# Expert gate and up products with the weight tiles held stationary and the tokens moving

## What is computed

```python
def expert_block(args):
    xb, e = args
    return (jax.nn.silu(xb @ w_gate[e]) * (xb @ w_up[e])) @ w_down[e]
```

## Time and profile before

| | |
|---|---|
| median of 3 runs | 1424.87 us |
| the profiled execution | 1424.23 us |
| its span, first to last instruction | 1422.5 us |
| PE busy | 1219.2 us, 86% of the span |
| weight loads busy | 919.9 us, 65% |
| DVE busy | 875.8 us, 62% |
| ACT busy | 739.7 us, 52% |
| mean granted TensorE clock | 0.949 |
| bytes moved | 285.04 MB |

### The profile page before, as it was taken

The page is one execution under the profiler, slowest core; times in us unless marked ns, Lnnn a source line. Parts: engine busy times, 40 slices in busy tenths (PEclk is TensorE's granted clock), DMA queues, the critical chain, the costliest instruction groups (busy, mean ns, idle before and its releaser), DMA issues. The chain is left out here.

```text
span 1422.5 us, 18503 instructions
## 1 busy us (share of the span) xinstructions
PE 1219.2 (86%) x6174; PEld 919.9 (65%) x6174; DVE 875.8 (62%) x951; ACT 739.7 (52%) x850; POOL 149.2 (10%) x140
## 2 busy tenths in 40 slices
PE   3799999999999999699824999999999999999700
PEld 2597678768767876488723666666666666666500
DVE  4334534453455345533375888888888888888525
ACT  5234344344334344522205777777777777777422
POOL 0000000000000000010002111111111111111043
PEclk9999999999999999899956999999999999999855
DMA  4121010111011110454345999999999999999256
GB/s 135 32 75 45 17 44 15 44 31 43 12 35 43 29 44 0 167 182 143 111 192 203 362 398 390 397 392 396 396 388 393 397 396 393 390 399 393 109 161 220
DMA packets 80460, 285.04 MB, mean 200 GB/s; under 512 B 12280, under 2 KB 38904, under 8 KB 55856
## 3 DMA queue, kind: packets, MB, share of 16 engines
q1 hardware_dynamic: 68384, 242.09, 45.0%
q0 software_dynamic: 8464, 30.02, 6.9%
q10 hardware_dynamic: 3584, 12.58, 2.2%
HBM read 255.01 MB, written 29.66 MB: 200 GB/s over the span
## 5 line engine op out<-in xcount | busy, mean ns | idle before, releaser
L1428 DVE TENSOR_TENSOR m_wl<-raw,m_wh 128x2048 fp32r<-128x2048 f32 x192 | 437.3, 2289 | 88.5 <-ACT m_wh L1372 86.2
L1372 ACT ACTIVATE m_wh<-raw 128x2048 fp32r<-128x2048 f32 x192 | 367.7, 1918 | 150.5 <-PE m_py L277 50.7
L289 PE MATMUL a_pj<-zh,a_wh 128*128 128x348 f32 (+1 forms) x432 | 112.0, 358 | 0.0
L289 PE MATMUL a_pj<-zl,a_wh 128*128 128x348 f32 (+1 forms) x432 | 111.8, 358 | 0.0
L289 PE MATMUL a_pj<-zh,a_wl 128*128 128x348 f32 (+1 forms) x432 | 110.7, 355 | 0.0
L275 PE MATMUL m_py<-m_wh,m_hh 128*96 128x512 f32 x256 | 103.6, 405 | 8.2 <-DVE m_hl L1457 8.2
L275 PE MATMUL m_pg<-m_wh,m_xh 128*96 128x512 f32 x256 | 104.6, 409 | 5.8 <-DVE m_xl L1432 4.4
L275 PE MATMUL m_pu<-m_wh,m_xh 128*96 128x512 f32 x256 | 102.6, 401 | 0.0
L277 PE MATMUL m_pg<-m_wh,m_xl 128*96 128x512 f32 x256 | 102.1, 399 | 0.0
L276 PE MATMUL m_py<-m_wl,m_hh 128*96 128x512 f32 x256 | 101.9, 398 | 0.0
L276 PE MATMUL m_pg<-m_wl,m_xh 128*96 128x512 f32 x256 | 101.8, 398 | 0.0
(11 more groups left out here) (259 smaller groups left out, 2139.1 us busy)
## 6 DMA issues: line engine op xcount, KB each, us to landing
raw<-in_w_gate_dram SPq DMA_DIRECT2D x64, 1024.0 KB, 8.1
raw<-in_w_up_dram SPq DMA_DIRECT2D x64, 1024.0 KB, 8.7
raw<-in_w_down_dram SPq DMA_DIRECT2D x64, 1024.0 KB, 7.7
a_raw<-in_w_in_dram SPq DMA_DIRECT2D x26, 512.0 KB, 3.8
yrows<-m_ys ACTq DMA_DIRECT2D x32, 384.0 KB, 7.7
yrows<-o_blank POOLq DMA_DIRECT2D x22, 384.0 KB, 4.5
a_cb<-negcum SPq DMA_DIRECT2D x8, 520.0 KB, 3.8
n_x<-in_x_dram SPq DMA_DIRECT2D x8, 512.0 KB, 3.2
```

Of the source, the lines that this page charges most:

```text
L289: mm = nc.tensor.matmul(out, w[:, k, 0:m], z[:, k, at:at + n], start=n_pass == 0, stop=n_pass == PASSES - 1)
L1372: nc.scalar.activation(wh[s][:], raw[j][:], ACT.Copy).then_inc(S["w_hi"], 1)
L1428: nc.vector.tensor_tensor(wl[s][:], raw[j][:], wh[s][:].bitcast(F32), ALU.subtract).then_inc(S["w_lo"], 1)
```

## The change

In gate and up the operands swap sides. The weights become stationary: of the 512 columns of a slice, tile m takes the columns m, m+4, m+8, ... (128 of them, every fourth), so that output partition p holds hidden column 4p+m, as `w_down` lies. The tokens move. Their high and low parts lie side by side in one buffer `xs`, and one matmul of `wh` against both gives 192 columns (96 for the high tokens, 96 for the low ones). A second matmul, of `wl` against the high part alone, adds its 96 columns to the first half. Per slice and for each of the four tiles m that is a pair of matmuls with two weight loads; before it was three matmuls with three weight loads for the whole slice.

The result has hidden columns on partitions already, so the four transposes to `phid` go. The two halves of each sum have to be added: ACT copies the second half out of PSUM (`low_g`, `low_u`), DVE adds the first half to it. Silu then works on the sum in SBUF. All these operations have 128 partitions and 384 elements.

```diff
-                            mm = three_passes(nc, out[:], xh[u][:, k * BLK:(k + 1) * BLK], xl[u][:, k * BLK:(k + 1) * BLK],
-                                              wh[s][:, n], wl[s][:, n], k == 0, k == KD - 1)
+                            for m in range(MT):
+                                n = slice(b * DE + m, (b + 1) * DE, MT)
+                                nc.tensor.matmul(out[:, spot(m):spot(m) + 2 * BLK], wh[s][:, n],
+                                                 xs[u][:, k, :, :].rearrange("p c n -> p (c n)"), start=k == 0 and m % 2 == 0, stop=False,
+                                                 skip_group_check=True)
+                                mm = nc.tensor.matmul(out[:, spot(m):spot(m) + BLK], wl[s][:, n], xs[u][:, k, 0, :],
+                                                      start=False, stop=k == KD - 1, skip_group_check=True)
...
-                        pe.wait_ge(S["silu_done"], N + 1)
+                        pe.wait_ge(S["g_summed"], N + 1)
                         into_hidden(N, u, pg, GATE, shift)
-                    if shift != FIRST:
                         pe.wait_ge(S["h_done"], N + 1)
-                        pe.wait_ge(S["h_lo"], N)
-                        for t in range(DE // P):
-                            mm = nc.tensor.transpose(phid[:, t * BLK:(t + 1) * BLK], hid[:, t * P:(t + 1) * P],
-                                                     c.ident[0:BLK, 0:BLK])
-                        mm.then_inc(S["h_turned"], 1)
-                    if shift != CLOSING:
                         into_hidden(N, u, pu, UP, shift)
```

On ACT (step N; `high` is the copy of one unit's high part):

```diff
                     if shift != CLOSING:
-                        for kind in GATE:
-                            high(N, u, kind + shift)
+                        high(N, u, GATE[0] + shift)
+                    if shift != FIRST:
+                        act.wait_ge(S["unit_used"], used(N - 1, UP[1], shift_of(N - 1) if isinstance(N, int) else INNER))
+                        act.wait_ge(S["h_done"], N)
+                        nc.scalar.activation(by_spot(low_u), sides(pu[:])[1], ACT.Copy).then_inc(S["u_copied"], 1)
+                        act.wait_ge(S["g_summed"], N + 1)
+                        nc.scalar.activation(act_g[:], act_g[:], ACT.Silu).then_inc(S["silu_done"], 1)
+                    if shift != CLOSING:
+                        high(N, u, GATE[1] + shift)
                         x_high(N, u)
...
                     if shift != FIRST:
+                        act.wait_ge(S["h_done"], N + 1)
...
+                        nc.scalar.activation(hh[:], hid[:], ACT.Copy).then_inc(S["h_hi"], 1)
                         for kind in DOWN:
                             high(N, u, kind + shift)
                     if shift != CLOSING:
                         act.wait_ge(S["unit_used"], used(N, GATE[1], shift))
-                        act.wait_ge(S["h_done"], N + 1)
-                        nc.scalar.activation(act_g[:], pg[:], ACT.Silu).then_inc(S["silu_done"], 1)
...
+                        act.wait_ge(S["g_summed"], N + 1)
+                        nc.scalar.activation(by_spot(low_g), sides(pg[:])[1], ACT.Copy).then_inc(S["g_copied"], 1)
```

More of the change, by code:

```diff
@@ L1249, in experts @@
         xg = [c.sb(ctx, f"{tag}_xg{s}", [BLK, D], F32) for s in range(2)]
-        xh = [c.sb(ctx, f"{tag}_xh{s}", [P, KD * BLK], F32R) for s in range(2)]
-        xl = [c.sb(ctx, f"{tag}_xl{s}", [P, KD * BLK], F32R) for s in range(2)]
+        xs = [c.sb(ctx, f"{tag}_xs{s}", [P, KD, 2, BLK], F32R) for s in range(2)]
         ids = [c.sb(ctx, f"{tag}_ids{s}", [BLK, 1], I32) for s in range(2)]
-        act_g = c.sb(ctx, tag + "_act_g", [BLK, DE], F32)
-        hid = c.sb(ctx, tag + "_hid", [BLK, DE], F32)
+        act_g = c.sb(ctx, tag + "_act_g", [P, DE // P * BLK], F32)
+        hid = c.sb(ctx, tag + "_hid", [P, DE // P * BLK], F32)
+        low_g = c.sb(ctx, tag + "_low_g", [P, DE // P * BLK], F32)
+        low_u = c.sb(ctx, tag + "_low_u", [P, DE // P * BLK], F32)
         hh = c.sb(ctx, tag + "_hh", [P, DE // P * BLK], F32R)
@@ L1375, in x_high @@
                     act.wait_ge(S["x_turned"], N + 2)
-                    nc.scalar.activation(tiles4(xh[u][:]), banks4(px[:]), ACT.Copy).then_inc(S["x_hi"], 1)
+                    nc.scalar.activation(part(u, 0), banks4(px[:]), ACT.Copy).then_inc(S["x_hi"], 1)
                 def y_out(i, u, k, down):
@@ L1395, in step @@
                     if shift != FIRST:
+                        act.wait_ge(S["h_done"], N + 1)
+                        if not (isinstance(N, int) and N == 1):
+                            act.wait_ge(S["unit_used"], used(N - 1, DOWN[1]))
+                        nc.scalar.activation(hh[:], hid[:], ACT.Copy).then_inc(S["h_hi"], 1)
                         for kind in DOWN:
@@ L1418, in _ @@
                 dve.sem_inc(S["x_lo"], 1)
+                dve.sem_inc(S["g_summed"], 1)
+                dve.sem_inc(S["u_summed"], 1)
                 dve.sem_inc(S["h_done"], 1)
@@ L1431, in x_low @@
                     dve.wait_ge(S["x_hi"], N + 1)
-                    nc.vector.tensor_tensor(tiles4(xl[u][:]), banks4(px[:]), tiles4(xh[u][:]).bitcast(F32),
-                                            ALU.subtract).then_inc(S["x_lo"], 1)
+                    nc.vector.tensor_tensor(part(u, 1), banks4(px[:]), part(u, 0).bitcast(F32), ALU.subtract).then_inc(S["x_lo"], 1)
                 def hidden(k):
[L1436 to L1441, removed]
+                    dve.wait_ge(S["u_copied"], k + 1)
+                    dve.wait_ge(S["h_lo"], k + 1)
+                    nc.vector.tensor_tensor(by_spot(hid), sides(pu[:])[0], by_spot(low_u), ALU.add).then_inc(S["u_summed"], 1)
+                    dve.wait_ge(S["u_summed"], k + 2)
+                    dve.wait_ge(S["silu_done"], k + 1)
+                    nc.vector.tensor_tensor(hid[:], hid[:], act_g[:], ALU.mult).then_inc(S["h_done"], 1)
                 def step(i, u, N, shift):
                     if shift != CLOSING:
-                        for kind in GATE:
-                            low(N, u, kind + shift)
+                        low(N, u, GATE[0] + shift)
                     if shift != FIRST:
@@ L1449, in step @@
                     if shift != CLOSING:
+                        low(N, u, GATE[1] + shift)
                         x_low(N, u)
```

36 lines of the change are left out of this document (19 added, 17 removed).

## The result

The changed kernel takes 2052.37 us (median of 4 runs, 2049.10 to 2053.20) against 1424.80 for the kernel before (now the median of 4 runs): ratio 1.4395, 95% interval 1.437 to 1.442. It is slower, as forecast. But the forecast was 1508 with a range up to 1970, so the size was missed by far.

What follows compares the result with a forecast made beforehand. PE was taken to bound the experts stage, with loads replacing columns as its pace: 1424.2 + 92.2 for gate and up - 8.6 for transposes = 1507.8, so 1508 us; own range 1495 to 1530, all cases 1494 to 1970.

Steps and rivals of the forecast that it cites:

- Rival C: Chain through ACT and DVE to xl becomes later than PE by 0.5 us a step: 16 us, 1524 us; chance 0.08.
- PE's former share: Sign in the profile after: the busy share of gate and up weight loads rises above 70%.
- the price of a load of 128 neighbouring columns: On PE in gate and up, 0.110 us a load sets the pace: +92.2 us over 64 products.
- Rival B: Gate and up loads hide and columns decide; the gain ends at the DMA engines: 1419 us; chance 0.06.
- I take no cost: Gate and up loads reading every fourth column, 16 bytes apart, stay at 0.110 us each, with nothing added for the stride.
- the upper bound: The stride at most doubles a gate or up load to 0.220 us: up to +451 us over 4096 loads.
- Rival A: The stride doubles gate and up loads to 0.220 us: 1959 us, step 34.6 us; chance 0.34 including values between.
- the clock: Granted clock in the experts stage: the forecast is wrong if it falls below 1.00; no time was assigned to it.
- the DMA engines as the next limit: If loads hide, DMA at share 1.01 limits the gain to at most 1% of the 573 us of 32 steps.

Runs made afterwards that it cites:

- block_columns: The changed kernel with each weight tile made of 128 neighbouring columns and w_down's rows fetched to match, so no load has a stride: 1537.92 us, ratio 1.0799.
- xl_first: The kernel before, without the swap, with DVE making the tokens' low part xl ahead of the hidden product: 1415.62 us, ratio 0.9942.
- moving_stride2: The kernel before, with the 512 moving weight columns of a gate or up matmul taken as every second one of two slices: 1761.43 us.
- wide_moving: The changed kernel, stride-four loads kept, with each gate and up matmul moving 512 token columns in place of 192 or 96: 2026.3 us.
- hid_in_a_row: The kernel before, without the swap, with the hidden product written without a stride and w_down's rows fetched to match: 1416.76 us, ratio 0.9952.

## Why the prediction was wrong

**Right: what bounds the kernel and which way it goes.** PE sets the pace in both kernels, the loads take over from the columns, and slower was forecast at 0.94. ACT and DVE stayed hidden, in block_columns too, whose step is close to the one forecast. Rival C is out by that run. (The 70% that the forecast calls PE's former share is that of the weight loads in the earlier trace rows; it is 95% after.)

**Right: the price of a load of 128 neighbouring columns.** 0.110 from three places of the trace; 0.1115 in block_columns, whose step of 20.61 us stands against the 20.5 of the forecast. The forecast of 1508 was in effect one for that kernel (1537.92), and even there 1530, the top of its own range, was passed, because of the clock in the first two steps. Rival B (loads that hide) is out by the same run.

**Wrong: "I take no cost" for the stride.** This is the step that failed. The argument was that a load already takes 0.86 ns per column and that a reader at half its full rate would keep up. It counted rates by columns. What is paid is 16-byte lines, at 1.82 ns each: 128 neighbouring columns have 32 lines (58 ns by that price, below the load's own 111), and every fourth column has 128 (233 ns). 4096 loads at +0.12 us is some 500 us.

**Wrong: the upper bound.** Rival A doubled the load, 0.220, to 1959 us. The mechanism and the place were right, its chance of 0.34 too low, and its size short: 0.2334 instead of 0.220 is 55 us, and the clock came on top. Its bound was a factor taken from DVE's writes. A bound was in reach from PE's own rows: 512 neighbouring float32 columns are 128 lines and take 0.231 us, and if lines were what is paid there, a load with 128 lines would cost about the same.

**Wrong: the clock was left out of the sum.** I named it only as something that would break the forecast. It cost 45 to 50 us in the token transposes and the down products. The loads of the changed kernel lost nothing to it, since their lines cost the same at either clock; those of block_columns lost 26 us in its first two steps. With slow loads and narrow moving operands this belonged beside rival A.

**Partly right: the DMA engines as the next limit.** They move the same bytes. That they would have come next in rival B is argued and not shown. At a share of 1.01 there was room for a step at least 1.3% shorter (17.91 to 17.67 us in xl_first), where I allowed 1%; where they do stop isn't known. The share is a poor measure of what is left: block_columns had 345 GB/s, as forecast (341), but at a share of 0.97 and not the 0.88 that the forecast scaled from the rate.

**Not settled.** Why a line costs 1.82 ns in a load and 1.77 in a moving operand, and why stride eight costs 0.006 us more than stride four. On the moving side only strides of one and two were run. The runs with strides of two, three and eight, moving_stride2 and wide_moving were run once each; what is read from them are spacings that repeat hundreds of times in a trace, but for the 17 at half clock in moving_stride2.

## What to carry to other kernels

Before operands are swapped, count three things for each side: moving columns, weight loads, and the 16-byte lines that each access touches. In this kernel's float32r products, the time from one matmul to the next was close to the largest of their prices. A stride of two in a stationary tile was nearly free, and a stride of four doubled the cost of a load; on the moving side a stride of two already doubled the cost of a matmul. If the layout asks for every fourth column, permute the rows of the next weight matrix in its fetch instead: that took 514 us off, and the other fetch cost nothing that could be measured (hid_in_a_row has it and is as fast as xl_first). The swap did not pay even so: block_columns is 8% slower than the kernel before.

An engine that starts "just in time" may be waiting. An overlap of two paths within 0.15 us in 17.9 was worth 0.6%, for an exchange of two lines.

## What the runs showed of the hardware

- A float32r weight load of 128 columns costs the larger of the engine's pace (0.1115 us at 2.4 GHz, 0.213 at 1.2 GHz) and its 16-byte lines at 1.82 ns: strides 1, 2, 3, 4, 8 gave 0.1115, 0.118, 0.176, 0.233, 0.239 us at full clock. The price of a line didn't change with the clock (0.233 at both with stride four).
- The moving operand costs 0.231 us for 512 neighbouring columns and 0.452 for every second one at full clock; at half clock it is 0.427 and 0.453.
- With 288 moving columns per pair of slow loads (0.467 us) the clock was 0.50 for most of a step; with 1024 in the same time it stayed at 1.00; with 288 per pair of loads at 0.111 it stayed at 1.00 too, once it was there, but came from 0.50 only 65 us into the stage (block_columns).
- Starts of matmuls aren't always the pace. In the earlier trace rows two starts lie 0.07 us apart where the loads allow 0.11; in block_columns the starts alternate and only a whole pair (0.223 us) shows the rate.
